# Nine dense layers as one stage, and a state-space model's output matrices made round by round

## The chip, the cores and the metric

The program runs on one core of a Trainium2 chip. The metric is the device time of one execution in microseconds. Names used here: TensorE (PE, with its weight loads PEld), VectorE (DVE), ScalarE (ACT), GpSimd (POOL), and SP, whose queue issues all the DMA.

## The reference

Two blocks of a network run one after the other on 1024 tokens of width 1024, all in float32. The first block puts 16 meta tokens ahead (1040 positions), normalizes, multiplies by a wide input matrix, and runs two mixers: a state-space mixer (s5) and a gated recurrence in heads (hgrn2). What matters here comes after:

```python
y = gelu(y)                                   # end of s5_mixer, its scan included
y_a = y * sigmoid(y @ w_glu)
merged = sigmoid(p5) * (y_a @ w_ssm_proj) + sigmoid(p6) * (y_b @ w_hgrn_proj)
h = h + merged @ w_out
z = rmsnorm(h, ffn_norm_g)
u = causal_dwconv(z @ w_up, conv_w, conv_b)   # 2 x 2816 columns, 3 taps
h = h + (silu(u[..., :2816]) * u[..., 2816:]) @ w_down
return rmsnorm(h[:, 16:], final_norm_g)
```

Inside the state-space mixer, every pair of groups needs the products of powers of its complex decay with its complex output matrix, `a^k * c` for k = 0 to 8. They are the matrix `ca` of the kernel. The second block (pooling, gating, attention, a Fourier mix) is not touched.

## The kernel before

Activations lie transposed: features on the 128 partitions, positions along the free axis, a layer of width 1024 as 8 tiles. Each fp32 product is made from three: operand and weight are split into a high part and a low part, and high x high, low x high, high x low are added up in PSUM. ScalarE writes the high part (a copy), VectorE the low part (a subtraction).

The order of stages around the change: `heads_out` (the projection of the second mixer, with the tables of the scan made beside it), `s5` (the scan), `gather`, nine calls of `dense`, `inverse_rms` between the third and the fourth, then `second_front`, whose names begin with joint. Every stage is a `Phase`: at its end all engines meet and its semaphores are cleared. So no engine begins the next stage until the last has finished.

- `heads_out`: 24 slots (8 output tiles x 3 slices of 342 positions) of 24 matmuls each. Two PSUM banks take turns: slot s waits until VectorE has evacuated slot s - 2 (`moved`). VectorE works through a list `at` that says in which slot each piece of the tables is made: `angles`, `power`, `coefficients`, `scaled_b`, then `outer` 0 to 8, each of six operations on 128 x 512 (all 32 pairs x 16), and `skip` after the last slot. GpSimd makes two turning tables there (`turn_table`, L879 to L884).
- `s5`: four rounds of 8 pairs. TensorE, in order, for round n: `kernel(n+1)`, `turn(n+1)`, `inputs(n+1, 0)`, `inputs(n+1, 1)`, then after `states` of n `outputs(n, 0)`, `inputs(n+1, 2)`, `outputs(n, 1)`. VectorE: `decays(n)`, `weights(n+1)`, `turned_back(n)`, `states_of(n)`. ScalarE copies the kernel blocks (`kernel_out`, L1319) and the transposes (`turn_out`), applies the gelu, and reorders finished tiles (`reorder`, L1349) from chunks to natural order. A tile makes this way through DRAM: stored in chunks, loaded, reordered, stored as `y_glu`. The reorder has two buffers on either side. `inputs(n, 2)` waits until `turned_back(n)` has left its first trip.
- `gather`: loads the 8 tiles of `y_glu` and splits them into the operand `xa`.
- `dense`: mt output tiles in a loop of pairs. Per tile and slice of 342 (or 512 for the down layers, which cover 1024 positions): kt x 3 matmuls. PSUM is two tiles of three banks. Weights have two stages (`stage`, shared by all layers, already loaded for the next layer by `following`), and two buffers for each part (`wh`, `wl`). An epilogue (`epi_...`) works on all the columns of a tile at once. TensorE's loop for a tile begins with these two waits:

```python
pe.wait_ge(low_ready, 2 * i + j + 1)
pe.wait_ge(psum_free, 2 * i + j + 1)
split_matmuls(pe, ps[j], wh[j], wl[j], x[0], x[1], kt, n, first).then_inc(psum_full, 1)
```

The layers in order, with tiles x kt: glu 8x8, ssm_proj 8x8, w_out 8x8, up0 16x8, down0 8x8, up1 16x8, down1 8x8, up2 12x8, down2 8x6. glu, w_out and the down layers read `xa`; ssm_proj and the up layers read `xb`. The up layers all read the same `xb`, so an up layer after a down layer needs nothing from it.

Of the kernel before, what the change touches and what calls it, by code (L numbers as in the profile page):

```python
# [19 lines left out]
P = 128  # L20
# [8 lines left out]
TAU = 8  # L29
# [100 lines left out]
def split_matmuls(pe, ps, wh, wl, xh, xl, kt, n, first):  # L130

    mm = None
    for b, c0, w in pieces(n):
        o = ps[:, 512 * b:512 * b + w]
        for k in range(kt):
            terms = ((wh, xh), (wl, xh), (wh, xl))
            for t, (a, x) in enumerate(terms):
                mm = pe.matmul(o, a[:, k * P:(k + 1) * P], x[:, k, first + c0:first + c0 + w],  # L138
                               start=(k == 0 and t == 0), stop=(k == kt - 1 and t == 2))
    return mm  # L140


def dense(nc, name, weights, mt, kt, x, n, epi, sides=(), side_at=None, store=None, extra=None, steps=(0, 0),
          off=0, stage=None, warm=False, following=None, first=0, pad=0):

    assert mt % 2 == 0
    weights = weights[off:off + mt]
    with Phase(nc, name) as ph:
        places = stage or [ph.sb(f"wstage{j}", (P, kt * P)) for j in range(2)]
        stage = [s[:, 0:kt * P] for s in places]
        early = 16 if warm else 0
        wh = [ph.sb(f"whigh{j}", (P, kt * P), F32R) for j in range(2)]
        wl = [ph.sb(f"wlow{j}", (P, kt * P), F32R) for j in range(2)]  # L160
        side = [[ph.sb(f"side{s}_{j}", (P, n)) for j in range(2)] for s in range(len(sides))]
        out = [ph.sb(f"out{j}", (P, n + pad)) for j in range(2)]
        ps = [ph.ps(f"psum{j}", (P, 1536)) for j in range(2)]
        zeroed = ph.sem("pad_zeroed")
        w_landed = [ph.sem(f"weights_landed{j}") for j in range(2)]
        side_landed = [[ph.sem(f"side{s}_landed{j}") for j in range(2)] for s in range(len(sides))]
        out_stored = [ph.sem(f"out_stored{j}") for j in range(2)]
        high_ready, low_ready = ph.sem("high_ready"), ph.sem("low_ready")
# [10 lines left out]
        act_epi, dve_epi = epi(e)  # L179
        half = mt // 2  # L180
        ns = len(sides)

        with nc.Block() as block:
            @block.sync
            def _(sp):
# [2845 lines left out]
```

## Time and profile before

| | |
|---|---|
| median of 3 runs | 3772.22 us (3770.91 to 3781.7) |
| the profiled execution: time, span | 3772.27 us, 3770.5 us |
| TensorE busy | 3351.4 us, 89% of the span |
| VectorE, ScalarE, GpSimd busy | 1994.3, 930.6, 294.9 us |
| mean granted TensorE clock | 0.935 |
| first matmul of glu, first of the stage after down2 | 1297.44 us, 2425.05 us |

Busy times are sums over the whole span. The granted clock is a share of 2.4 GHz, and in the table of stretches its two levels show as 1.00 and 0.50, or a mixture. A TensorE that is busy is not always one at its peak: records overlap, so work per matmul is better read from counts over a stretch. Times of rows are microseconds from the start of the span.

### The profile page before, as it was taken

The page shows a single profiled execution, that of the slowest core. Times are in us where ns is not written, and L with a number is a line of the kernel's source. Part 1 is how long each engine was busy: PE and PEld are TensorE (multiplying, and loading weights), DVE is VectorE, ACT ScalarE, POOL GpSimd, SP SyncE. Part 2 cuts the span into 40 slices and gives each one's busy share as a digit, 9 for nine tenths or more (in the row PEclk, how much of TensorE's full clock was granted, in tenths as well). Part 3 has the DMA queues.
Part 4 walks back from the last instruction along what each step waited for, and adds up shares of the span by engine and source line. Part 5 has one row for each costly group of instructions (what it writes and reads, how often), then busy time and mean ns, then how long its engine had stood idle before and what let it go on. Part 6 is the DMA issues. An engine that isn't in the chain of part 4 may idle for free. (4 is left out here: it accounts for less than half of the span.)

```text
span 3770.5 us, 48109 instructions
## 1 busy us (share of the span) xinstructions
PE 3351.4 (89%) x19662; PEld 3016.3 (80%) x19662; DVE 1994.3 (53%) x2626; ACT 930.6 (25%) x1143; POOL 294.9 (8%) x327
## 2 busy tenths in 40 slices
PE   3999999997878599899899898899988977999787
PEld 3999999997866499899789788799988974555445
DVE  5566566564877134556246345645445536666236
ACT  3222222222223211121011001222133314444213
POOL 0000000000536000000000000000022001222100
PEclk9999999998988599999999999999989988999998
DMA  2322222322353423311311311411121330000221
GB/s 95 96 87 77 74 91 86 96 85 97 128 61 86 135 95 123 112 45 45 123 50 45 106 67 50 144 41 41 49 82 36 136 127 1 1 1 1 91 77 68
DMA packets 102120, 287.36 MB, mean 76 GB/s; under 512 B 13120, under 2 KB 31936, under 8 KB 101568
## 3 DMA queue, kind: packets, MB, share of 16 engines
q1 hardware_dynamic: 101952, 285.03, 23.4%
q8 instruction: 117, 1.92, 0.2%
q14 instruction: 51, 0.42, 0.0%
HBM read 221.00 MB, written 63.98 MB: 76 GB/s over the span
## 5 line engine op out<-in xcount | busy, mean ns | idle before, releaser
L756 PE MATMUL mixer_in_dense<-mix_z_high,mixer_in_whigh 128*128 128x348 f32 x1344 | 443.6, 330 | 11.3 <-POOL mixer_in_out L593 11.3
L756 PE MATMUL mixer_in_dense<-mix_z_high,mixer_in_wlow 128*128 128x348 f32 x1344 | 436.6, 325 | 0.0
L756 PE MATMUL mixer_in_dense<-mix_z_low,mixer_in_whigh 128*128 128x348 f32 x1344 | 435.8, 324 | 0.0
L1888 PE MATMUL joint_dense<-rst_norms_operand_b_high,joint_whigh 128*128 128x342 f32 (+2 forms) x1056 | 344.9, 327 | 18.2 <-DVEq L2005 10.1
L138 PE MATMUL up_psum<-rst_norms_operand_b_high,up_whigh 128*128 128x342 f32 x1056 | 341.1, 323 | 21.5 <-DVE up_wlow L262 21.5
L1888 PE MATMUL joint_dense<-rst_norms_operand_b_high,joint_wlow 128*128 128x342 f32 (+2 forms) x1056 | 341.7, 324 | 0.0
L1888 PE MATMUL joint_dense<-irst_norms_operand_b_low,joint_whigh 128*128 128x342 f32 (+2 forms) x1056 | 340.6, 323 | 0.0
L138 PE MATMUL up_psum<-irst_norms_operand_b_low,up_whigh 128*128 128x342 f32 x1056 | 339.7, 322 | 0.0
L138 PE MATMUL up_psum<-rst_norms_operand_b_high,up_wlow 128*128 128x342 f32 x1056 | 339.6, 322 | 0.0
L756 PEld LDWEIGHTS mixer_in_dense<-mix_z_high,mixer_in_whigh 128*128 128x128 f32 x1344 | 257.5, 192 | 13.1 <-POOL mixer_in_out L593 11.9
L756 PEld LDWEIGHTS mixer_in_dense<-mix_z_high,mixer_in_wlow 128*128 128x128 f32 x1344 | 256.7, 191 | 0.8
L756 PEld LDWEIGHTS mixer_in_dense<-mix_z_low,mixer_in_whigh 128*128 128x128 f32 x1344 | 256.3, 191 | 0.0
L1888 PEld LDWEIGHTS joint_dense<-rst_norms_operand_b_high,joint_whigh 128*128 128x128 f32 x1056 | 202.3, 192 | 23.8 <-DVEq L2005 8.0
L138 PEld LDWEIGHTS up_psum<-rst_norms_operand_b_high,up_whigh 128*128 128x128 f32 x1056 | 201.8, 191 | 23.3 <-DVE up_wlow L262 23.3
L1888 PEld LDWEIGHTS joint_dense<-irst_norms_operand_b_low,joint_whigh 128*128 128x128 f32 x1056 | 203.2, 192 | 0.0
L1888 PEld LDWEIGHTS joint_dense<-rst_norms_operand_b_high,joint_wlow 128*128 128x128 f32 x1056 | 202.7, 192 | 0.6 <-issue 0.5
L138 PEld LDWEIGHTS up_psum<-rst_norms_operand_b_high,up_wlow 128*128 128x128 f32 x1056 | 201.7, 191 | 0.0
L138 PEld LDWEIGHTS up_psum<-irst_norms_operand_b_low,up_whigh 128*128 128x128 f32 x1056 | 201.0, 190 | 0.0
L138 PE MATMUL down_psum<-first_operand_a_high,down_whigh 128*128 128x512 f32 x352 | 140.9, 400 | 33.6 <-DVE down_wlow L262 33.6
L2357 PEld LDWEIGHTS attn_turned<-all_ident,attn_probs 128*128 128x128 f32 x640 | 75.3, 148 | 94.1 <-DVE attn_turned_probs L2496 36.4
L138 PE MATMUL down_psum<-first_operand_a_low,down_whigh 128*128 128x512 f32 x352 | 141.5, 402 | 0.0
L138 PE MATMUL down_psum<-first_operand_a_high,down_wlow 128*128 128x512 f32 x352 | 139.6, 397 | 0.0
(548 smaller groups left out, 6906.0 us busy)
## 6 DMA issues: line engine op xcount, KB each, us to landing
mixer_in_wstage<-w_in SPq DMA_DIRECT2D x56, 512.0 KB, 4.7
mixer_in_mod_w<-w_mod SPq DMA_DIRECT2D x64, 384.0 KB, 3.6
first_norms_weights<-w_up SPq DMA_DIRECT2D x44, 512.0 KB, 3.5
down_side<-h SPq DMA_DIRECT2D x24, 512.0 KB, 4.2
h<-down_out SPq DMA_DIRECT2D x24, 512.0 KB, 2.9
first_norms_weights<-ab_w_in SPq DMA_DIRECT2D x20, 512.0 KB, 3.5
p<-mixer_in_out SPq DMA_DIRECT2D x16, 528.0 KB, 2.9
first_norms_weights<-w_down SPq DMA_DIRECT2D x16, 512.0 KB, 4.9
```

The lines of the kernel that those rows point to most:

```text
L138: mm = pe.matmul(o, a[:, k * P:(k + 1) * P], x[:, k, first + c0:first + c0 + w], start=(k == 0 and t == 0), stop=(k == kt - 1 and t == 2))
L756: mm = pe.matmul(pd[s % 2][:, 0:W], a[n % 2][:, P * m:P * (m + 1)], z[x][:, m, W * b:W * (b + 1)], start=m == 0 and i == 0, stop=m == DT - ...
L1888: mm = pe.matmul(pd[s % 2][:, 0:wide], a[n % 2][:, P * k:P * (k + 1)], m, start=k == 0 and e == 0, stop=k == DT - 1 and e == 2)
L2357: mm = pe.transpose(o[:, 256 * kk + P * ab:256 * kk + P * ab + P], pr[(2 * s + ab) % 3][:, c0:c0 + P], c["ident"][:, :])
```

## The change

Two edits.

1. `dense`, `gather`, the epilogues and the inverse root after w_out are replaced by one function `dense_flow`, one phase with an unrolled program over all 100 output tiles. Every tile has three slices of 342 positions (340 in the last of a down layer), which go through a ring of six PSUM banks (`RING`). The weight parts have three buffers (`NW`), and their split runs two tiles ahead. At the start of each layer TensorE goes through the six slices of its first two tiles k by k, and waits for operand tile k only when it comes to it (`operand`); in every other tile it goes slice by slice. VectorE evacuates slice by slice and does the rest of the epilogue after the third. The first operand is loaded and split in the same phase. The sums of squares for the inverse root are three fp32 products inside up0, and the root is made per slice.
2. In `heads_out` the output matrices `ca` are made for round 0 alone, in slots 11 to 13, and `skip` in slot 15. The other rounds' are made in `s5` by VectorE, ahead of `weights(n+1)`. The powers and the output matrices are kept in SBUF for that, and `reorder` in `s5` has one buffer on either side instead of two.

```diff
+def outer_part(ch, tt, ca, re, im, cr, ci, n, nq, k, m, t1, t2):
+    pairs, shape = slice(nq * n, nq * (n + 1)), [P, nq, m, SG]
...
+    ch.inc(tt(u, r, a, ALU.mult))
+    ch.do(tt(v, i, b, ALU.mult))
+    ch.do(tt(ca[:, pairs, 0, k:k + m, :], u, v, ALU.add))
+    ch.inc(tt(u, i, a, ALU.mult))
+    ch.do(tt(v, r, b, ALU.mult))
+    ch.do(tt(ca[:, pairs, 1, k:k + m, :], u, v, ALU.subtract))
...
-                       (8, "coefficients", 0), (9, "reverse", 0), (9, "scaled_b", 0), (10, "negate", 0), (10, "outer", 0),
-                       (12, "outer", 1), (13, "outer", 2), (15, "outer", 3), (16, "outer", 4), (18, "outer", 5),
-                       (19, "outer", 6), (21, "outer", 7), (22, "outer", 8), (NS, "skip", 0)):
+                       (8, "coefficients", 0), (9, "reverse", 0), (9, "scaled_b", 0), (10, "negate", 0), (11, "outer", 0),
+                       (12, "outer", 4), (13, "outer", 8), (15, "skip", 0)):
...
-                            ch.do(ts(pw[:, 2, :, :], pw[:, 1, :, :], -1.0, None, ALU.mult))
+                            ch.inc(dve.tensor_copy(ends_re[:, :, :], pw[:, 0, :, :]))
+                            ch.do(ts(ends_im[:, :, :], pw[:, 1, :, :], -1.0, None, ALU.mult))
...
-        a, b = ([ph.sb(f"{n}{j}", (P, T1)) for j in range(2)] for n in ("chunked", "natural"))
+        a, b = ([ph.sb(f"{n}{j}", (P, T1)) for j in range(1)] for n in ("chunked", "natural"))
...
+                def fetch(m):
+                    if m:
+                        sp.wait_ge(moved, m)
+                    sp.dma_start(a[0][:, :], t["y_chunks"][m]).then_inc(landed, 16)
...
                     if n:
                         put(2 * n - 2)
+                        fetch(2 * n - 1)
                         put(2 * n - 1)
                     for par in range(2):
                         sp.wait_ge(stored[par], 16 * TAU * (n + 1))
-                    for m in (2 * n, 2 * n + 1):
-                        sp.dma_start(a[m % 2][:, :], t["y_chunks"][m]).then_inc(landed[m % 2], 16)
+                    fetch(2 * n)
                 put(DT - 2)
+                fetch(DT - 1)
                 put(DT - 1)
...
                 def kernel(n):
                     pe.wait_ge(spread, n + 1)
+                    if n:
+                        pe.wait_ge(outer_ready, n)
...
                     decays(n)
                     if n + 1 < ROUNDS:
+                        for k in (0, TAU):
+                            outer_part(ch, tt, ca, ends_re, ends_im, cr, ci, n + 1, NQ, k, TAU if k == 0 else 1, t1, t2)
+                        dve.sem_inc(outer_ready, 1)
                         weights(n + 1)
```

The core of `dense_flow` (n is a tile, s a slice, b = s % 3; `free(s)` waits for the evacuation of slice s - 6):

```diff
+    W, RING, NW = NM // 3, 6, 3
...
+            @block.sync
+                load(0)
+                for m in range(4):
+                    sp.dma_start(ring[m][:, :], t["y_glu"][m][:, FIRST:FIRST + NM]).then_inc(y_landed[m], 16)
+                    if m == 0:
+                        load(1)
...
+                for n in range(NTILE):
+                    if n and n - 1 in store_at:
+                        put(n - 1)
+                    nxt = [m for m in sided if m > n]
+                    if n and n - 1 in side_at and side_at[n - 1] + 2 < len(sided):
+                        load_side(sided[side_at[n - 1] + 2])
+                    if n + 4 < NTILE + 2:
+                        sp.wait_ge(low_ready, n + 3)
+                        load(n + 4)
...
+            @block.tensor
+                for l, (name, members, kt) in enumerate(layers):
+                    n0, x = start_of[l], reads[name]
+                    six = range(3 * n0, 3 * n0 + 6)
+                    for k in range(kt):
+                        pe.wait_ge(operand, operand_base[name] + k + 1)
+                        if name == "up0" and k == kt - 1:
+                            pe.wait_ge(acc_ready, 1)
+                            square_sum(0)
+                            square_sum(1)
+                        for s in six:
+                            if k == 0:
+                                free(s)
+                                if s % 3 == 0:
+                                    pe.wait_ge(low_ready, s // 3 + 1)
+                            mm = products(s, k, kt, x)
+                            if k == kt - 1:
+                                mm.then_inc(full, 1)
+                    if name == "up0":
+                        pe.wait_ge(rooted, 1)
+                        square_sum(2)
+                    for s in range(3 * n0 + 6, 3 * (n0 + len(members))):
+                        free(s)
+                        if s % 3 == 0:
+                            pe.wait_ge(low_ready, s // 3 + 1)
+                        for k in range(kt):
+                            mm = products(s, k, kt, x)
+                        mm.then_inc(full, 1)
...
+            @block.scalar
+                def high(n):
+                    act.wait_ge(w_landed[n % 2], 16 * (n // 2 + 1))
+                    if n >= NW:
+                        act.wait_ge(full, 3 * (n - NW + 1))
...
+                for s in range(NS):
...
+                    if b == 0 and n + 2 < NTILE:
+                        high(n + 2)
...
+            @block.vector
+                for s in range(NS):
...
+                    if b == 1 and n + 2 < NTILE:
+                        low(n + 2)
...
+                    elif kind == "up":
+                        j = i % 2
+                        dve.wait_ge(full, s + 1)
+                        if n < start_of[3] + 2:
+                            dve.wait_ge(rooted, 2 * b + 2)
+                        mvd.do(tt(v[j][:, at], bank, rms[:, where], ALU.mult))
+                        if b < 2:
+                            continue
...
+                        ch.do(ts(out[j][:, 0:SEQ], v[j][:, 2:], tap(2), tap(3), ALU.mult, ALU.add))
+                        for e in (1, 0):
+                            ch.do(stt(out=out[j][:, 0:SEQ], in0=v[j][:, e:e + SEQ], scalar=tap(e), in1=out[j][:, 0:SEQ],
+                                      op0=ALU.mult, op1=ALU.add))
+                        if j == 0:
+                            dve.sem_inc(conv_ready, 1)
+                        else:
+                            dve.wait_ge(silued, pair_at[n] + 1)
+                            ch.do(tt(out[1][:, 0:SEQ], other[0][:, 0:SEQ], out[1][:, 0:SEQ], ALU.mult))
+                            write(xa, (n - start_of[layer_of[n]]) // 2, seq, out[1][:, 0:SEQ])
```

## Rows read from the trace of the kernel before

**Rows 1.** Stretches: us; busy us of each engine; granted clock; DMA share, GB/s.
```profile
1071.00:1252.00 181.00, 156.35 (x1004) 125.46 (x1003) 113.40 (x128) 59.46 (x116) 75.63 (x104) 0.81 0.37 68
...
1297.00:2416.00 1119.00, 1036.52 (x5958) 986.03 (x5958) 537.33 (x482) 163.07 (x158) 0.00 (x0) 0.95 0.24 82
```
**Rows 2.** Waits of TensorE: who waited for whom, us in total, times, longest.
```profile
PE down_psum L138 <- DVE down_wlow L262: 33.6, 3, 11.4
...
PE up_psum L138 <- DVE up_wlow L262: 21.5, 3, 7.4
...
PE heads_out_dense L1033 <- DVE heads_out_out L1153: 12.3, 5, 4.9
...
PE ffn_rms_sum L315 <- PEq L101: 9.6, 1, 9.6
...
PE w_out_psum L138 <- DVE w_out_wlow L262: 9.1, 1, 9.1
...
PE ssm_proj_psum L138 <- DVE ssm_proj_wlow L262: 7.7, 1, 7.7
```
**Rows 3.** Stretches inside up0 and down0, and glu's first 5.5 us.
```profile
1617.00:1795.00 178.00, 178.00 (x1136) 178.00 (x1135) 108.34 (x95) 31.52 (x29) 0.00 (x0) 1.00 0.13 42
...
1820.00:1897.00 77.00, 77.00 (x336) 62.98 (x335) 15.93 (x13) 6.37 (x6) 0.00 (x0) 1.00 0.38 129
...
1297.00:1302.50 5.50, 5.06 (x18) 5.06 (x19) 1.61 (x2) 2.34 (x2) 0.00 (x0) 0.50 0.57 177
```
**Rows 4.** Timeline of TensorE: start, us, instruction; idle time before it, releaser.
```profile
1297.44 0.65 PE L138 MATMUL glu_psum<-first_operand_a_high,glu_whigh 128*128 128x342 f32 x1 [45.45 <-DVE glu_wlow L262]
...
2425.05 3.75 PE L1833 MATMUL joint_pooled<-first_norms_inverse_rms,all_ones 128*128 128x512 f32 x4 [9.60 <-PEq L101]
```
**Rows 5.** Timeline of ScalarE at the seam between up0 and down0.
```profile
1804.35 2.00 ACT L240 ACTIVATE down_whigh<-first_norms_weights 128x1024 fp32r<-128x1024 f32 x2 [14.20 <-PEq L101]
```
**Rows 6.** Timeline of SP's queue and ScalarE in gather.
```profile
1271.09 10.39 SPq L1459 DMA_DIRECT2D gather_a<-y_glu  x8
...
1274.77 1.08 ACT L1465 ACTIVATE first_operand_a_high<-gather_a 128x1056 fp32r<-128x1056 f32 x1 [7.72 <-DMA gather_a<-y_glu]
```
**Rows 7.** Timeline of SP's queue and ScalarE at the scan's end.
```profile
1258.01 1.44 SPq L1214 DMA_DIRECT2D scan_chunked<-y_chunks  x2
...
1265.13 2.28 SPq L1196 DMA_DIRECT2D y_glu<-scan_natural  x2
...
1263.05 4.00 ACT L1349 ACTIVATE scan_natural<-scan_chunked 128x1056 f32<-128x1056 f32 x2 [6.74 <-DMA scan_chunked<-y_chunks]
```
**Rows 8.** heads_out: TensorE from slot 11 on; one of VectorE's outer products.
```profile
988.40:1055.30 66.90, 55.31 (x312) 0.90 0.22 77
...
1005.16 1.66 DVE L1133 TENSOR_TENSOR s_ca<-heads_out_t 128x512 f32<-128x512 f32 x1
```
**Rows 9.** The scan: timeline of VectorE, TensorE and SP; two stretches of outputs.
```profile
1120.66 1.23 DVE L884 TENSOR_TENSOR scan_wt<-scan_t 128x1024 f32<-128x1024 f32 x1
...
1123.47 0.56 DVE L1413 TENSOR_TENSOR scan_ei<-scan_v,s_w_im 128x396 f32<-128x396 f32 x1
...
1126.83 1.12 PE L1269 MATMUL scan_v<-scan_u,scan_win 128*64 128x132 f32 x16
...
1178.38 0.90 SPq L1196 DMA_DIRECT2D y_glu<-scan_natural  x2
...
1221.31 0.81 PE L1282 MATMUL scan_y<-scan_u,scan_toeplitz 128*128 128x132 f32 x2 [6.44 <-DVEq L1434]
...
1196.40:1205.20 8.80, 8.80 (x50) 6.75 (x48) 4.50 (x9) 1.00 (x2) 0.00 (x0) 0.97 0.00 0
...
1221.20:1252.10 30.90, 30.68 (x96) 23.04 (x96) 0.00 (x0) 2.46 (x6) 0.00 (x0) 0.50 0.26 75
```
**Rows 10.** Timeline of GpSimd in the scan's turning tables.
```profile
1114.68 1.20 POOL L879 TENSOR_TENSOR scan_pool_t<-s_w_re 128x8 f32<-128x8 f32 x1
...
1160.32 0.21 POOL L879 TENSOR_TENSOR scan_pool_t<-s_w_re 128x8 f32<-128x8 f32 x1
```

More of the change, by code:

```diff
@@ L127, in loop @@
         self.n = base + trips * per
[L130 to L140, printed above, removed]
@@ L1444, in _, with flow_tiles @@
                     states_of(n)
-def gather(nc, name, src, x):
-    with Phase(nc, name) as ph:
-        a = [ph.sb(f"a{j}", (P, T1)) for j in range(4)]
-        landed = [ph.sem(f"landed{j}") for j in range(4)]
-        high_ready, low_ready = ph.sem("high_ready"), ph.sem("low_ready")
+def flow_tiles():
+    layers = [("glu", [("glu", m) for m in range(DT)], DT), ("ssm", [("ssm", m) for m in range(DT)], DT),
+              ("out", [("out", m) for m in range(DT)], DT)]
+    first = 0
+    for f, k in enumerate((8, 8, 6)):
+        layers.append((f"up{f}", [("up", 2 * first + i) for i in range(2 * k)], DT))
+        layers.append((f"down{f}", [(f"down{f}", m) for m in range(DT)], k))
+        first += k
+    return layers
@@ new lines, in put @@
+                def put(n):
+                    q, (kind, i) = store_at[n], tiles[n]
+                    first, size = (META, SEQ) if kind.startswith("down") else (FIRST, NM)
+                    sp.wait_ge(out_ready, q + 1)
+                    sp.dma_start(t["h"][i][:, first:first + size], out[q % 2][:, 0:size]).then_inc(out_stored[q % 2], 16)
+                load(0)
[3 more added lines that the diff above has]
+                        load(1)
@@ new lines, in _ @@
+                for m in range(4, DT):
+                    sp.wait_ge(operand, m - 3)
+                    sp.dma_start(ring[m % 4][:, :], t["y_glu"][m][:, FIRST:FIRST + NM]).then_inc(y_landed[m % 4], 16)
+                for n in (2, 3):
+                    sp.wait_ge(low_ready, n - 1)
+                    load(n)
+                load_side(0)
+                load_side(1)
+                for n in range(NTILE):
[7 more added lines that the diff above has]
+                        load(n + 4)
@@ new lines, in _, with low, write @@
+                tt, stt, ts = dve.tensor_tensor, dve.scalar_tensor_tensor, dve.tensor_scalar
+                def low(n):
+                    dve.wait_ge(high_ready, n + 1)
+                    w = kt_of[n] * P
+                    tt(wl[n % NW][:, 0:w], stage[n % 2][:, 0:w], wh[n % NW][:, 0:w].bitcast(F32),
+                       ALU.subtract).then_inc(low_ready, 1)
+                def write(x, m, where, src):
+                    ch.do(split(dve, ch, x[0][:, m, where], x[1][:, m, where], src))
+                    dve.sem_inc(operand, 1)
```

520 lines of the change are left out of this document (217 added, 303 removed).

## The prediction

> **What bounds the kernel now.** I read the table of stretches first. In the nine dense layers (1297 to 2416 us) TensorE is busy 1036 of 1119 us while VectorE is busy 537 and DMA a quarter of the time [rows 1]: TensorE sets this stage's end, and only its idle time, its slow clock and its time per matmul can be shortened. Second, the waits of TensorE [rows 2]: inside the stage they are 7.7, 9.1, 9.6, 21.5 (three times) and 33.6 (three times), 81.5 us in nine pauses, one at each seam between layers and one before the inverse root. Third, the same table over pieces inside one layer [rows 3]: at full clock (2.4 GHz) 1136 matmuls of 342 columns take 178 us, 0.1567 us each; 336 of 512 columns take 77 us, 0.229 each; after a pause 18 matmuls take 5.06 us at half clock (1.2 GHz), 0.281 each. Fourth, the stage's ends [rows 4]: the first matmul of glu starts at 1297.44 after 45.45 idle, the last of down2 ends at 2425.05 - 9.60 = 2415.45. So the stage lasts 1118.0 us.
>
> Ahead of it lie heads_out and the scan. In the scan TensorE is busy 156 of 181 us but at clock 0.81, and VectorE 113 [rows 1]: two engines take turns there, neither has much room.
>
> **The nine layers as one stage.** What goes: eight ends of a phase. At such a seam ScalarE starts splitting the new weights, already landed, only once everybody has finished, 1804.35 where the last matmul ended near 1795.3 [rows 5]. Now weights are split two tiles ahead into three buffers, beside the matmuls, so the pause has no cause left but a late operand. The operand's tail (evacuate, convolve, gate, split) ends before that 1804.35, so it is at most 9 us long. Over it TensorE has seven of eight slices k for the first two tiles, 7 x 18 x 0.157 = 19.7 us (down2: five of six, 14.1). Covered; without that cover each seam would cost up to 9 us again.
>
> The work itself: 4896 matmuls of 342 columns stay, 1056 of 512 become 1584 of about 341. Together 6480 x 0.1567 = 1015.4 us; today's shares are 767 and 242, so the narrower tiles give back 6. One slow start remains, 18 x (0.281 - 0.157) = 2.3. The sums of squares stay, three fp32 products; four records of 512 columns take 3.75 at half clock [rows 4], so I take 3.5 with the short wait for the first inverse root. The roots are now three pairs with a table load each, but beside 2.8 us of matmuls and with slices 1 and 2 needed 3.8 and 7.5 us later. Stage: 1015.4 + 2.3 + 3.5 = 1021.2 against 1118.0, **-96.8**. VectorE's busy share in up is 108 of 178 us [rows 3], 6.8 us per 11.3 us tile; three short evacuations for one long one add some 0.4. Six banks give two tiles of slack, and after a k-by-k start VectorE has two tiles' work (about 15 us) before TensorE needs, 11 us on, the bank of the second tile's first slice. I keep -80 as the poor end (two us per seam), -99 as the good one. The unrolled program adds no row that I can point to; the scan and the mixer before are unrolled too.
>
> The end of the stage: the last evacuation covers a third of the columns, and the last store leaves before the norm's work instead of after it. Of the 9.60 us [rows 4] I take **-2** (0 to -4).
>
> **The gather.** Today eight tiles are loaded and split, the phase ends, weights are loaded, and the first matmul comes 26.35 us after the first load was issued (1271.09) [rows 4, 6]. Now the first weights go out first, and product k starts when tile k is split. The first load lands 3.7 us after issue, eight take 10.4 us to issue, 1.3 each [rows 6]; then 1.1 on ScalarE [rows 6] and 1.3 on VectorE (1.23 for 1024 columns, [rows 9]): 3.7 + 1.3 + 1.1 + 1.3 = 7.4. After that a k costs TensorE 18 x 0.28 = 5.1 us at half clock, and data come every 1.5: no starving. **-19** (-21 to -15).
>
> **The end of the scan.** The buffers of the reorder go from two to one. Today both loads go out at 1258.01, the first lands at 1263.05, two reorders take 4.00, and the stores go out at once; the gather starts 3.7 after the last [rows 7]. Now each of the last three tiles is load (4.2), reorder (2.0), next load: 3 x 6.6 = 20 from 1256.6, plus 3.7: 1280.3. **+9** (+5 with loads of 3 us, +12 with 5).
>
> **heads_out.** Of 54 operations on 512 columns for the outer products 12 of 512 and 6 of 128 remain, early (slots 11 to 13), and the skip matrix moves under the matmuls. From the twelfth slot on, 312 matmuls take 66.9 us [rows 8]; 13 x 24 x 0.1567 is 48.9. The surplus is waits for VectorE's evacuations (12.3 us over the stage [rows 2]) and the half clock after them. The pieces left are still beside GpSimd's tables, where such an operation takes up to 1.66 us [rows 8]; the three slots with them keep about 4 us. **-14** (-18 to -9).
>
> **The scan's rounds.** Three rounds get 12 new VectorE operations each: six of 1024 columns at 1.23 [rows 9] and six of 128, with overlap 7.4 + 1.5 = 8.9 us, ahead of weights and turned_back. In round 0 VectorE idles longer than that: free. In round 1 it does not: weights end at 1121.89 and turned_back follows at once; its first trip's last read of PSUM ends at 1124.03, and will end 8.9 later. TensorE's third inputs wait for that trip; they started at 1126.83 without a wait, 2.8 us after it [rows 9]. So TensorE pauses 6.2 us. How that ends is seen once in this trace: after 6.44 idle at 1221.31 the clock is at half and stays there for the whole 30.9 us of outputs, 15.4 per half against 8.8 at full [rows 9]. If it goes so here: 6.2 + 6.7 for the half + 2.4 until the next kernel products = 15.3, and round 2's own lateness of VectorE (two rounds' 17.8, less slack) is then hidden behind TensorE. If the clock holds: 6.2 + about 5.5 in round 2. Then ScalarE: after a round's gelus its second reorder now waits for a load that SP issues behind eight stores (the put before is at 1178.38 [rows 9]), some 6 us, and the copies of round 3's Toeplitz blocks are queued behind it; TensorE's transposes wait for those: +4.8, and perhaps 7 more at half clock. Sum: 11.7 + 4.8 = 16.5 or 15.3 + 4.8 + 0 to 7. I take **+20**; ends +8 (rounds absorb half) and +32.
>
> GpSimd's first table in that stretch shows 1.20 us for an operation on 8 columns beside VectorE's two-input operations, 0.21 alone [rows 10]. It has one such operation per VectorE operation, so 12 new ones hold it 9 us longer per round; round 3's turned_back, which waits for the last table, would then be late by a few us, inside the +32. The Trainium skill (SBUF — State Buffer, SBUF: two separate sides) says that whichever of the two starts first has the shared port pair for the whole instruction and the other blocks. By that rule, with both rounds' delays added up, the sum would be some 4 us higher; the trace agrees on the single operation.
>
> **Sum.** -96.8 - 2 - 19 + 9 - 14 + 20 = -102.8. The profiled execution took 3772.27 (span 3770.5), the median is 3772.22, so the two can be set equal: 3772.2 - 102.8 = 3669.4, **3669 us**.
>
> **Rivals.** (a) The banks are late: VectorE's burst after each k-by-k start, plus the single v and gate buffers, leave about 4 us at each of nine seams. For it: two tiles complete together and VectorE must do the convolution of both. Against: 15 us of work against 22 us of matmuls. 3669 + 36 = 3705.
> (b) The scan takes the worst of all its branches and GpSimd's table is last: +13, 3682; inside the range.
> (c) The weights or operands are late after all (SP's one queue holds a store's wait ahead of the next weights), so most seams stay: 60 of the 81.5 us come back, 3730 to 3745. Against: a weight load lands two tiles, 22 us, ahead.
> (d) Slower: in a k-by-k start the six banks change every three matmuls. If TensorE idles a little at each change, the clock falls as it does in the scan, and 8 x 144 + 108 = 1260 matmuls cost 0.281 instead of 0.157: +156, 3825. It decides once two thirds of them run at half clock (103 of the 156 us). Against it: the scan's kernel products change place every few matmuls, and the stretch 1071 to 1252 still has 0.81. The Trainium skill (TensorE: Matmul & The Clock Gate, A second HAM failure mode: psum-queue depth-cycling) tells of a kernel whose cycling through banks kept the clock oscillating; no row here shows it for products of 342 columns.
> (e) The change doesn't do what it says, the program stays bound by the same pauses: excluded for the most part, since no phase ends are left in the stage.
>
> **Chances.** Forecast with its own scatter 0.73, (a) 0.12, (b) 0.08, (c) 0.03, (d) 0.03, (e) 0.01. The terms' ends alone would add up to 3642 and 3711, unlikely all together. Leaving out (c), (d), (e), the upper half of (a) and some 6 in 100 at the low end gives 3645 to 3700. A measurement of this kernel can tell about 0.3% (11 us) from no change: all but (d) and (e) are faster by more, 0.96; same 0.01; slower 0.03.
>
> **What would show it.** Right: TensorE has no wait over 3 us between the first glu matmul and the last of down2, and that stage lasts 1017 to 1030 us at clock 0.99 or more; glu starts 7 to 8 us after the first load; heads_out's last 13 slots take about 53 us; the scan shows a new wait of TensorE for VectorE inside round 0's outputs and a longer one before round 3's transposes, and lasts 15 to 30 us more, tail included. Wrong: waits on the banks' semaphore in up layers, low clock in the first 22 us of each layer, or a scan that grows by less than 10 or more than 40.

## The result and the profile after

The changed kernel takes **3683.76 us** (median of 4 runs, 3683.07 to 3684.67) against 3774.57 us of the kernel before on the same chip: ratio 0.9759, 95% interval 0.9744 to 0.9775. The forecast was 3669 with a range of 3645 to 3700. The profiled executions differ by 3681.3 - 3770.5 = -89.2 us of span, and by TensorE's timeline that comes from these parts (first matmuls, the last gelu and the first load of y are the marks):

| part | before | after | change | forecast |
|---|---|---|---|---|
| up to heads_out's first matmul | 926.1 | 928.4 | +2.3 | 0 |
| heads_out, first to last matmul | 129.1 | 119.1 | -10.0 | -14 |
| scan, first matmul to last gelu | 185.7 | 207.2 | +21.5 | +20 |
| last gelu to first load of y | 18.7 | 29.6 | +10.9 | +9 |
| first load to first matmul of glu | 26.4 | 7.0 | -19.4 | -19 |
| nine layers | 1118.0 | 1022.7 | -95.3 | -96.8 |
| stage exit | 9.6 | 6.4 | -3.2 | -2 |
| from the next stage's first matmul to the end | 1345.4 | 1349.4 | +4.0 | 0 |

(The fixed 11.5 us between heads_out and the scan is in neither row.) The first and the last row are scatter: the profiles of the changed kernel and of the twelve below, none of which touches these stages, have heads_out start between 922.7 and 932.5, and the last part takes 1337 to 1349 us. So 6.3 of the 13.6 us by which the sum of the profile misses the forecast belong to no step. The stages between scatter too. In the seven kernels whose scan is that of the changed kernel it takes 207.2 to 212.2 us, and the scan of the kernel before takes 185.7 here and 187.9 in `flow_alone` below; heads_out takes 118.9 to 120.8 in seven kernels with the changed one, 129.1 and 130.5 with the old.

TensorE's waits, of the changed kernel (who waited for whom, total us, times, longest):

```profile
PE flow_dense L1344 <- DVEq L1457: 37.0, 1, 37.0
...
PE scan_turned_and_kernel L1002 <- ACT scan_toeplitz L1070: 17.0, 5, 5.6
...
PE scan_v L1020 <- DVEq L1165: 9.8, 2, 6.5
...
PE heads_out_dense L784 <- DVE heads_out_out L899: 5.0, 4, 3.4
...
PE flow_dense L1344 <- DVE flow_wlow L1436: 0.4, 1, 0.4
```

Against the nine pauses of [rows 2] the layers show one wait of 0.4 us, besides the 37.0 ahead of the stage. The table of stretches (us; busy of PE, PEld, DVE, ACT, POOL; granted clock; DMA share, GB/s), for heads_out from slot 11, a piece behind the scan's new pause, the scan's last outputs, and the whole dense stage:

```profile
990.70:1047.50 56.80, 52.60 (x312) 51.50 (x312) 31.47 (x39) 7.44 (x7) 46.57 (x79) 0.94 0.25 89
...
1127.70:1149.30 21.60, 21.60 (x83) 16.94 (x82) 21.03 (x19) 1.39 (x3) 20.81 (x17) 0.52 0.15 26
...
1235.00:1266.00 31.00, 30.68 (x96) 23.02 (x96) 0.00 (x0) 4.67 (x7) 0.00 (x0) 0.50 0.27 73
...
1302.70:2325.50 1022.80, 1022.30 (x6486) 1020.88 (x6486) 568.55 (x655) 169.38 (x180) 0.00 (x0) 1.00 0.28 95
```

TensorE is busy 1022.3 of 1022.8 us there at clock 1.00, with VectorE at 569: nothing but the count of matmuls is left. The two lines of the scan are at half clock. Timeline of TensorE at the marks and the new waits (start, us, ..., idle before and releaser):

```profile
1006.03 0.65 PE L784 MATMUL heads_out_dense<-heads_out_yb_high,heads_out_whigh 128*128 128x342 f32 x1 [3.40 <-DVE heads_out_out L899]
...
1125.69 2.03 PE L1020 MATMUL scan_v<-scan_u,scan_win 128*64 128x132 f32 x16 [6.50 <-DVEq L1165]
...
1198.43 1.09 PE L1002 MATMUL scan_turned_and_kernel<-all_ident,scan_wt 128*128 128x128 f32 x4 [5.65 <-ACT scan_toeplitz L1070]
...
1201.86 1.54 PE L1002 MATMUL scan_turned_and_kernel<-all_ident,scan_wt 128*128 128x128 f32 x6 [2.34 <-ACT scan_toeplitz L1070]
...
1302.75 0.65 PE L1344 MATMUL flow_dense<-first_operand_a_high,flow_whigh 128*128 128x342 f32 x1 [37.00 <-DVEq L1457]
...
2331.91 2.90 PE L1847 MATMUL joint_pooled<-first_norms_inverse_rms,all_ones 128*128 128x512 f32 x3 [6.42 <-PEq L101]
```

And SP's queue at the end of the scan, where [rows 7] showed two loads and two stores in pairs:

```profile
1270.35 0.43 SPq L945 DMA_DIRECT2D scan_chunked<-y_chunks  x1
...
1277.68 0.32 SPq L940 DMA_DIRECT2D y_glu<-scan_natural  x1
1278.11 0.37 SPq L945 DMA_DIRECT2D scan_chunked<-y_chunks  x1
1284.52 0.32 SPq L940 DMA_DIRECT2D y_glu<-scan_natural  x1
1284.88 0.43 SPq L945 DMA_DIRECT2D scan_chunked<-y_chunks  x1
1291.40 0.32 SPq L940 DMA_DIRECT2D y_glu<-scan_natural  x1
...
1295.72 0.42 SPq L1304 DMA_DIRECT2D flow_side<-y_glu  x1
```

A load (4.3 us from issue to landing), the reorder on ScalarE (2.06) and the issue of its store (0.4) take 1284.88 - 1278.11 = 6.8 us per tile and stand in a row three times; nobody waits there for the store to land. The next stage's first load leaves at 1295.72, and glu starts 7.03 later.

### The profile page after: what moved, and what is told of

Read it like the earlier page. It is cut to its first block and busy times, and to the rows that moved or that the text cites. A ratio compares the mean times of both kernels' runs of the same rounds, so it can differ in the third digit from the quotient of the medians.

```text
span 3681.3 us, 47804 instructions
## 1 busy us (share of the span) xinstructions
PE 3348.9 (91%) x20190; PEld 3059.9 (83%) x20190; DVE 2014.9 (55%) x2795; ACT 930.9 (25%) x1159; POOL 294.2 (8%) x327
## 5 line engine op out<-in xcount | busy, mean ns | idle before, releaser
L1344 PE MATMUL flow_dense<-rst_norms_operand_b_high,flow_whigh 128*128 128x342 f32 x1248 | 399.2, 320 | 0.4 <-DVE flow_wlow L1436 0.4
L1344 PE MATMUL flow_dense<-irst_norms_operand_b_low,flow_whigh 128*128 128x342 f32 x1248 | 398.3, 319 | 0.0
L1344 PE MATMUL flow_dense<-rst_norms_operand_b_high,flow_wlow 128*128 128x342 f32 x1248 | 397.4, 318 | 0.0
L1902 PE MATMUL joint_dense<-rst_norms_operand_b_high,joint_whigh 128*128 128x342 f32 (+2 forms) x1056 | 344.8, 326 | 17.9 <-DVEq L2019 10.1
L1344 PE MATMUL flow_dense<-first_operand_a_high,flow_whigh 128*128 128x342 f32 (+1 forms) x912 | 291.9, 320 | 37.0 <-DVEq L1457 37.0
L1344 PE MATMUL flow_dense<-first_operand_a_low,flow_whigh 128*128 128x342 f32 (+1 forms) x912 | 292.4, 321 | 0.0
L1344 PE MATMUL flow_dense<-first_operand_a_high,flow_wlow 128*128 128x342 f32 (+1 forms) x912 | 291.7, 320 | 0.0
L491 PEld LDWEIGHTS mixer_in_dense<-mix_z_high,mixer_in_whigh 128*128 128x128 f32 x1344 | 258.1, 192 | 13.6 <-POOL mixer_in_out L328 12.3
L1344 PEld LDWEIGHTS flow_dense<-rst_norms_operand_b_high,flow_whigh 128*128 128x128 f32 x1248 | 235.1, 188 | 1.3 <-issue 1.2
L1344 PEld LDWEIGHTS flow_dense<-rst_norms_operand_b_high,flow_wlow 128*128 128x128 f32 x1248 | 235.1, 188 | 0.1
L1344 PEld LDWEIGHTS flow_dense<-irst_norms_operand_b_low,flow_whigh 128*128 128x128 f32 x1248 | 234.5, 188 | 0.0
L1344 PEld LDWEIGHTS flow_dense<-first_operand_a_high,flow_whigh 128*128 128x128 f32 x912 | 172.9, 190 | 37.3 <-DVEq L1457 37.3
```

Of the source, the lines that this page charges most:

```text
L491: mm = pe.matmul(pd[s % 2][:, 0:W], a[n % 2][:, P * m:P * (m + 1)], z[x][:, m, W * b:W * (b + 1)], start=m == 0 and i == 0, stop=m == DT - ...
L1344: mm = pe.matmul(o, w[n % NW][:, P * k:P * (k + 1)], x[h][:, k, where], start=k == 0 and e == 0, stop=k == kt - 1 and e == 2)
L1902: mm = pe.matmul(pd[s % 2][:, 0:wide], a[n % 2][:, P * k:P * (k + 1)], m, start=k == 0 and e == 0, stop=k == DT - 1 and e == 2)
```

## The experiments

All times are medians; each kernel has 4 runs (the last one 5) beside the kernel before on the same chip, and the interval is that of the ratio to it. Profiles are of one execution each.

### The two edits apart

`flow_alone`: the new dense stage, with `heads_out`, `s5` and `keep` of the kernel before. `ssm_alone`: the reverse.

> The one-stage dense layers with heads_out and the scan of the kernel before. If the two edits act one after the other and add up, this run gets heads_out's old 129.1 us back (+10.1 against the changed kernel) and loses the scan's and its tail's 32.4: 3683.8 - 22.3 = 3661 us, flow stage still 1023 us, first glu matmul 7 us after the first load. Rival: the state-space edit is neutral and the changed kernel's scan is longer only because its stage starts earlier: 3680 or more.

> The state-space edit with the gather and the nine dense phases of the kernel before. Additive theory: slower than before by 22, 3774.6 + 22.3 = 3797 us, with the same scan as in the changed kernel (TensorE's waits of 6.5 and 5.65 us in it). Rival (edit neutral): 3775 within 4.

Measured: flow_alone 3659.51 us (ratio 0.9702, 0.9681 to 0.9723), ssm_alone 3798.05 (1.0063, 1.0043 to 1.0084). In flow_alone the scan takes 187.9, its tail 19.2, glu starts 7.4 after the first load and the layers take 1021.4. The edits add up. The dense stage is worth 3659.51 - 3776.82 = -117, and the state-space edit by itself costs +21 to +24: it gives 10 us in heads_out and loses 32 in the scan and its tail.

### What makes the dense stage free of pauses

`late_split`: at each of the eight seams the new layer's first two weights are split after the old layer's last tile; no phase ends come back.

```diff
-                    if b == 0 and n + 2 < NTILE:
+                    if b == 0 and n and n in start_of:
+                        act.wait_ge(full, 3 * n)
+                        high(n)
+                        high(n + 1)
+                    if b == 0 and n + 2 < NTILE and n + 2 not in start_of and n + 1 not in start_of:
                         high(n + 2)
```

(and `low` on VectorE likewise)

> The changed kernel, but at each of the eight seams the weights of the new layer's first two tiles are split only after the old layer's last tile is finished on ScalarE and VectorE (the phase ends stay away). Theory 1 (a seam's pause in the kernel before was the split of the weights queued behind the last epilogue, not the meeting of the engines as such): each seam waits for epilogue tail (0.5 to 8 us) + 1.1 on ScalarE + 1.2 on VectorE, so 3 to 10 us, and starts at half clock where it is long: about +50, 3734 us (+35 to +75). Theory 2 (it was the phase end: drain, meeting, clearing): under +15, 3699 or less.

Measured: 3746.14 (0.993, 0.9911 to 0.9949), the layers 1088.2 instead of 1022.7, +65.5. TensorE at two seams, and the stretch behind the first:

```profile
1403.29 0.63 PE L1344 MATMUL flow_dense<-rst_norms_operand_b_high,flow_whigh 128*128 128x342 f32 x1 [5.38 <-DVE flow_wlow L1440]
...
1797.60 0.62 PE L1344 MATMUL flow_dense<-first_operand_a_high,flow_whigh 128*128 128x342 f32 x1 [8.88 <-DVE flow_wlow L1440]
...
1403.30:1408.30 5.00, 5.00 (x18) 5.00 (x19) 0.98 (x1) 1.50 (x2) 0.00 (x0) 0.50 0.82 297
```

The eight waits are 5.38, 5.51, 7.54, 8.88, 2.50, 8.88, 2.50 and 8.61, together 49.8. Behind seven of the eight the clock stays at half for another 3.9 to 5.9 us, 33 us in all (18 matmuls in 5.00 us instead of 2.8), which costs half of that; 49.8 + 16.5 = 66.3 accounts for the 65.5. Theory 1 holds. Of the nine pauses of [rows 2] eight are at these seams, 71.9 us; the ninth, 9.6, is the inverse root's. So 71.9 - 49.8 = 22 us, some 3 a seam, are left for the phase ends themselves.

`slices`: TensorE takes the first six slices one after the other (`for s, k in ((s, k) for s in six for k in range(kt))`), only the first of them with the waits for each k.

> The changed kernel, but TensorE goes slice by slice in the first two tiles of a layer too; only its first slice is taken k by k. Theory 1 (the k-by-k start over six banks is what covers an operand's tail): after the last matmul of a layer the tail still takes about 3.7 us after glu and ssm_proj, 5.5 after w_out and 8 after an up layer, of which 3.3 are covered: waits of 0.5, 0.5, 2 and three of 5, with 2.3 of half clock after each of the last three, together +25: 3709 us (+15 to +40). Theory 2 (only the merging counts; the order of k is idle): 3684 within 4.

Measured: 3717.16 (0.9853, 0.9831 to 0.9875), the layers 1058.4, +35.7. A seam, and the start of glu:

```profile
1785.68 0.65 PE L1344 MATMUL flow_dense<-first_operand_a_high,flow_whigh 128*128 128x342 f32 x1 [4.17 <-DVEq L1442]
...
1304.70:1325.00 20.30, 15.35 (x48) 12.31 (x49) 11.00 (x9) 10.21 (x10) 0.00 (x0) 0.52 0.74 268
```

The same stretch of late_split, whose glu also starts at 1304.67:

```profile
1304.70:1325.00 20.30, 20.30 (x113) 20.30 (x114) 11.05 (x9) 10.55 (x10) 0.00 (x0) 0.87 0.77 274
```

The six waits at seams with a new operand are 0.68, 0.81, 2.85, 4.17, 4.18 and 5.11 (expected 0.5, 0.5, 2, 5, 5, 5), 17.8 together. What was not expected is glu's start, where the operand's tiles are still being split one by one: four waits of 4.5 us together and half clock until 1324.0, 48 matmuls in 20.3 us. late_split, which starts as the changed kernel does, has 113 there, so it costs 65 x 0.157 = 10 us. With 2.3 of half clock after the three long waits that makes 35. Theory 1 holds, its size at the upper end of the range.

`one_tile`: `six = range(3 * n0, 3 * n0 + 3)`, the k-by-k start over three banks; the slices taken one by one begin three earlier.

> The changed kernel, but the k-by-k start spans three banks (the first tile of a layer), not six. It covers 7 x 9 x 0.157 = 9.9 us of an operand's tail (7.1 before down2) instead of 19.7. The slice-by-slice run measured the tails as its waits plus 3.3: 4.0, 4.1, 6.1, 7.5, 7.5 and 7.5 us. Theory (cover is a count of matmuls against the tail): no wait over 1 us, 3684 us within 4. Rival (the start over two tiles is needed, since VectorE must also evacuate six full banks in time or the weights of the second tile are late): 1 to 3 us at each of eight seams, 3692 to 3708.

Measured: 3682.47 (0.9753, 0.9732 to 0.9774), no change from 3683.76; the layers take 1023.4 and the waits inside the stage add up to 1.3 us. A cover of 9.9 us over tails up to 7.5 is enough.

### The end of the scan

`tail`: er and ei are second buffers of the reorder for tiles 5 and 7.

```diff
+        a, b = [a[0][:, :], flat(ei)], [b[0][:, :], flat(er)]
+        buf = [0, 0, 0, 0, 0, 1, 0, 1]
```

> The changed kernel, but tiles 5 and 7 of the scan's reorder use er and ei (free by then) as second buffers. Theory: the scan's tail (last gelu to first load of y) is a chain of load, reorder, load, so it goes back from 29.6 to 18.7 us and nothing else moves: 3683.8 - 10.9 = 3673 us. Rival: the tail is bound by the stores of the last chunks and by the phase end, and two of its tiles through the same queue gain 4 or less: 3680.

Measured: 3675.25 (0.9736, 0.9715 to 0.9756). The last gelu to the first load takes 24.0 us (29.6 with one buffer): half of what was expected. That the total came within 3 us of the expected 3673 all the same is scatter of other stages. The load of tile 5 was queued behind the 16 chunk stores, which SP issues until 1270.55; issued between their halves (in `best`, below) it brings the tail to 19.4. So the chain is the cause, and SP's queue was a second link in it.

### Where the scan's 21 us come from

`trips`: in rounds 1 and 2 VectorE takes turned_back's first two trips, then the output matrices, the third trip, and the weights last.

> The changed kernel, but in rounds 1 and 2 VectorE takes trips 0 and 1 of turned_back before the output matrices, trip 2 after them, and the weights last. Theory (the 6.5 us pause of TensorE inside round 0's outputs is VectorE's order, and the half clock of the next 33 us is the pause's consequence): no wait over 1 us there, clock 0.95 or more from there to round 3's transposes, -16.6: 3667 us. Rival 1: the pause goes but the clock stays at half anyway: -6.5, 3677. Rival 2: the wait only moves to the matrices or the weights of round 2, now later by 7 us: 3675 to 3684, with a new wait of TensorE for VectorE before the kernel products or the transposes of round 2.

Measured: 3682.88 (0.9762, 0.9741 to 0.9783), no gain: rival 2, with its new wait of 2.68 us before round 2's transposes. TensorE, and two stretches:

```profile
1152.05 0.81 PE L1033 MATMUL scan_y<-scan_u,scan_toeplitz 128*128 128x132 f32 x2 [4.97 <-DVEq L1185]
...
1125.00:1139.00 14.00, 12.01 (x96) 9.84 (x94) 13.50 (x14) 6.22 (x15) 13.37 (x12) 1.00 0.35 77
...
1152.10:1188.00 35.90, 35.90 (x130) 27.61 (x130) 34.48 (x40) 4.89 (x7) 33.71 (x46) 0.50 0.13 23
```

The pause inside round 0's outputs is gone and the clock there is 1.00. But states(1) is late: 4.97 us right before round 1's outputs, and half clock for all of the 36 us behind it. VectorE's list of that round takes 47.3 us (from the decays at 1104.61 to the end of the states at 1151.94), 45.2 in the changed kernel, and TensorE's own work in a round is 37. The 39 us that the expectation below gives VectorE leave out what its operations lose beside GpSimd's table, which is made at the same time. Two instructions of the changed kernel, the same operation in rounds 0 and 1:

```profile
1099.59 1.24 DVE L1178 TENSOR_TENSOR scan_t<-scan_ei,s_w_im 128x1048 f32<-128x1048 f32 x1
...
1142.31 2.10 DVE L1178 TENSOR_TENSOR scan_t<-scan_ei,s_w_im 128x1048 f32<-128x1048 f32 x1
```

`round2_home`: round 2's matrices in heads_out (`(17, "outer", 32), (19, "outer", 36), (21, "outer", 40)`, the number is 16 x round + k), none in the scan's round 1.

> The changed kernel, but the output matrices of round 2 are made in heads_out (slots 17, 19 and 21), not in the scan's round 1. The run before this one showed that putting VectorE's work of round 1 in another order only moves TensorE's pause: in round 1 VectorE has 39 us of work against TensorE's 37. Theory (amount, not order): with 8.9 us less in that round TensorE's pause inside round 0's outputs goes from 6.5 to below 1, the half clock after it too: -16.6, and the three pieces cost heads_out 1 to 3 us: 3684 - 16.6 + 2 = 3669 us. Rival (the half clock belongs to this part of the scan whatever VectorE does): -6.5 + 2, 3679.

Measured: 3682.33 (0.9757, 0.973 to 0.9783). Heads_out takes 121.0 (+1.9, as expected) and the pause in round 0's outputs is gone, yet the scan takes 205.5. TensorE one round later:

```profile
1166.01 0.71 PE L1021 MATMUL scan_v<-scan_u,scan_win 128*64 128x132 f32 x4 [4.76 <-DVEq L1166]
...
1117.00:1143.00 26.00, 26.00 (x185) 20.79 (x184) 24.60 (x27) 6.55 (x15) 24.35 (x32) 1.00 0.31 63
...
1166.00:1186.00 20.00, 19.99 (x77) 15.51 (x78) 18.81 (x20) 3.51 (x4) 18.98 (x20) 0.50 0.08 14
```

Round 3's matrices, which VectorE makes in its round 2 and which the changed kernel hid behind a TensorE at half clock, now stop it for 4.76 inside round 1's outputs, and the clock falls there instead.

`scan_free` and `best`: round 2's matrices stay in heads_out, those of rounds 1 and 3 are both made in the scan's round 0, with turned_back ahead of the weights there; ScalarE's second reorder moved behind the next round's transposes; `best` has the tail's buffers too.

```diff
+                        for q in ((1, 3) if n == 0 else ()):
...
+                        if n:
+                            dve.sem_inc(outer_ready, 1)
+                        else:
+                            turned_back(n)
                         weights(n + 1)
```

> The changed kernel with round 2's output matrices in heads_out, round 1's and round 3's in the scan's round 0 (where VectorE had 10 us idle before turned_back; turned_back stands ahead of the weights there), and ScalarE's second reorder of a round moved behind the next round's transposes. The run before showed that one round with too much VectorE work is enough: with round 2's share gone the pause moved to round 2 (4.8 us, then half clock) and the scan still took 205.5 us from first matmul to last gelu. Theory (every added wait over about 4 us costs itself and some 10 us of half clock, and there is nothing else in the scan's loss): without any of them the scan takes 186 again, as before the change (185.7), against 207.2: 3684 - 21 + 2 for heads_out = 3665 us. Rival: GpSimd's tables or ScalarE's copies take over as the late one: 3675 or more.

> The same, and er and ei as second reorder buffers for tiles 5 and 7, with the load of tile 5 issued between the two halves of the last chunk stores (in the run that used these buffers it stood behind all 16, and the tail took 24.0 us, not 18.7). Theory: tail 19 to 20 us, so 3665 - 10 = 3655 us, below the dense layers alone with the old state-space code (3659.5). Rival: the tail stays at 24: 3659.

Measured: scan_free 3677.92 (0.9741, 0.9719 to 0.9762), scan 204.1, the theory failed; best 3669.68 (0.9735, 0.9709 to 0.9761) and not 3655, scan 201.6, with the tail of 19.4 that was expected. The theory of the "wait over about 4 us" is wrong. scan_free:

```profile
1111.73 0.59 PE L1034 MATMUL scan_y<-scan_u,scan_toeplitz 128*128 128x132 f32 x1 [2.89 <-DVEq L1188]
...
1111.80:1149.00 37.20, 37.20 (x134) 28.57 (x135) 31.23 (x33) 2.79 (x6) 34.92 (x48) 0.50 0.16 28
...
1149.00:1158.00 9.00, 9.00 (x64) 7.53 (x62) 2.66 (x4) 3.80 (x9) 7.59 (x28) 0.80 0.25 70
```

Right before the outputs stands a wait of 2.89 us, and half clock for the whole 37 us behind it. It isn't shown that 2.89 us do this by themselves: in both kernels a wait of 4.01 us ends 12 us earlier, before the transposes, the clock is at half after that one too, and it has been back for only 3.4 us when it falls again. No run has so short a wait alone there. ScalarE's part did work: before round 3's transposes TensorE waits 3.00 again, not 5.65 and 2.34.

`no_pause`: `best` with the changed kernel's order in round 0 (matrices, weights, turned_back).

> As the run before with all parts (round 2's matrices in heads_out, the others' in round 0, ScalarE's second reorder later, er and ei as buffers, early load of tile 5), but VectorE's order in round 0 is again that of the change: matrices of rounds 1 and 3, then the weights, then turned_back. There the scan still took 201.6 us (204.1 without the buffers), though no wait of TensorE before the last round was over 4.01 us: turned_back ahead of the weights had put a wait of 2.9 to 3.3 us right before round 0's outputs, and the clock stood at half for the 36 us behind it. Theory (what costs is a pause right before or inside the outputs, of 2.9 us as well as of 6.5; a wait of 3.0 before the transposes gives the clock back within 7 us): with none in rounds 0 to 2 the stretch from round 0's outputs to round 1's Toeplitz wait lasts 40 us at clock over 0.9, the scan 187 us: 3670 - 14.5 = 3655 us. Rival (the amount of VectorE work moved into round 0 is the cause, by a later states(0)): the same wait stands before round 0's outputs again, scan over 198 us, 3667 or more.

Measured: **3651.53** (5 runs, 3643.67 to 3655.1; ratio 0.9661, 0.9644 to 0.9677), scan 188.3, tail 19.2, heads_out 121.5. The theory holds. The amount of VectorE work is that of `best`, and only the place of the wait differs:

```profile
1091.73 0.49 PE L1030 MATMUL scan_v<-scan_u,scan_win 128*64 128x132 f32 x2 [4.86 <-DVEq L1177]
...
1096.00:1103.00 7.00, 7.00 (x60) 5.93 (x58) 6.71 (x9) 3.30 (x8) 0.00 (x0) 0.98 0.00 0
...
1114.00:1148.00 34.00, 31.23 (x225) 25.10 (x222) 31.44 (x33) 9.50 (x23) 32.04 (x39) 0.95 0.24 48
```

TensorE waits 4.86 us ahead of round 0's third inputs, followed by the kernel products: clock 0.98 within 5 us. Its outputs have no wait ahead, and 34 us with them pass at 0.95. The wait before round 1's transposes differs too, 4.01 us in best and 3.00 here, as in the changed kernel. This kernel beats the change and also flow_alone; the intervals of its ratio and of flow_alone's (from 0.9681) don't meet. Its scan and tail are back at flow_alone's (187.9 and 19.2), and it keeps 9 us in heads_out (121.5 against 130.5).

### heads_out

`spread`: round 0's three pieces in slots 11, 13, 15, the skip matrix in 17.

> The changed kernel, but heads_out's three output-matrix pieces of round 0 stand in slots 11, 13 and 15 and the skip matrix in 17, not in 11, 12, 13 and 15. Theory: the missing 4 us of heads_out (56.8 us from slot 11 on, not 52.9) are the queue of two pieces of 5 and 7 us in slots that last 3.8 each: the waits of 3.4 and 0.7 go, with the half clock after them: -5, 3679 us. Rival: beside GpSimd's tables every piece is longer than two slots, and the waits only move: 3684.

Measured: 3680.45 (0.9758, 0.9737 to 0.9779; single runs 3670.77 to 3686.32); heads_out 118.3 against 119.1, less than the scatter. The rival: the waits moved. Two of VectorE's instructions there and TensorE's wait after them:

```profile
1004.96 1.54 DVE L654 TENSOR_TENSOR heads_out_t<-s_powers_re,s_c_im 128x512 f32<-128x512 f32 x1
...
1008.00 2.18 DVE L806 TENSOR_TENSOR heads_out_wlow<-heads_out_wstage,heads_out_whigh 128x1024 fp32r<-128x1024 f32 x1
...
1010.75 0.62 PE L784 MATMUL heads_out_dense<-heads_out_yb_high,heads_out_whigh 128*128 128x342 f32 x1 [2.95 <-DVE heads_out_out L899]
```

Beside GpSimd's table the split of a weight takes 2.18 us (1.23 alone), so a slot's own work grows as well as the piece.

## Why the prediction was right, point by point

- **The nine layers as one stage** (-96.8, measured -95.3): right in mechanism and size. 6480 x 0.1567 = 1015.4 is what a busy TensorE does; 7.3 us remain for the slow start, the sums and 0.4 of waiting, where I had 5.8. That split weights two tiles ahead take away the seam is shown (late_split, +65.5), that the k-by-k start covers the operand's tail too (slices, +35.7), and the cover has room (one_tile, 0). Rivals (a), (c), (d) and (e) are excluded: no bank waits, no late weights, clock 1.00 through the stage, starts over six banks included. (The Trainium skill, in TensorE: Matmul & The Clock Gate, A second HAM failure mode: psum-queue depth-cycling, tells of a clock that went up and down while matmuls cycled through banks; it was named beside (d), and no run here shows it.)
- **Stage exit** -3.2 (forecast -2) and **gather** -19.4 (-19): inside their ranges, the gather as worked out; 7.0 us from load to matmul against 7.4.
- **The scan's rounds** (+20, measured +21.5): the first pause is 6.50 (forecast 6.2). From round 1's third inputs, which stand inside round 0's outputs, to round 2's transposes the scan lost 10.1 us to half clock (forecast 9.1). Round 2's lateness hid behind it, as assumed, and round2_home shows it uncovered. Before round 3's transposes the waits are 5.65 and 2.34 instead of 2.99: +5.0 (forecast 4.8). All three steps stand. That the terms agree so closely is luck in part: in the seven kernels with this scan the first pause is 5.04 to 6.76 us and the scan grows by 19 to 27. That half clock costs more than the pause was already in the sum; the experiments add where a pause brings it. The working on GpSimd was off: 12 operations at 0.99 us each are 11.9 us a round, not 9, and the two tables together took 91.6 us instead of 80.8. They were done at 1197.52, and round 3's turned_back began at 1208.52, released by TensorE, so they made nothing late there. What the sum had not seen is VectorE's side, its operations of up to 2.1 us instead of 1.24.
- **The scan's end** (+9, measured +10.9): three cycles, to the end of the last store's issue, took 1291.72 - 1270.35 = 21.4 us instead of 20, the first landing 5.2 us after issue and not 4.2, and the first load of y follows by 4.0 us, not 3.7; the first weights of glu are issued ahead of it. The stated bound of 15 to 30 us for scan and tail together was 2 us too narrow (32.4).
- **heads_out** (-14, measured -10.0): right in sign, mis-sized by 4. I kept 4 us for the three slots with pieces; they cost 56.8 - 48.9 = 7.9. The pieces took 5.0, 6.8 and 5.5 us. The last was thought small, six operations on 128 columns. Three of them, and two of GpSimd's at that time:

```profile
1006.40 0.28 DVE L651 TENSOR_TENSOR heads_out_t<-s_powers_negated_im,s_c_im 128x128 f32<-128x128 f32 x1
1006.72 1.26 DVE L652 TENSOR_TENSOR s_ca<-heads_out_t 128x128 f32<-128x128 f32 x1
1008.01 1.10 DVE L653 TENSOR_TENSOR heads_out_t<-s_powers_negated_im,s_c_re 128x128 f32<-128x128 f32 x1
...
1006.41 1.41 POOL L616 TENSOR_TENSOR s_w_re<-heads_out_pool_t 128x512 f32<-128x512 f32 x1
1007.90 1.06 POOL L617 TENSOR_TENSOR heads_out_pool_t<-s_w_re,s_w_im 128x512 f32<-128x512 f32 x1
```

The same form takes 0.28 alone, and the last four of the piece take 1.10 to 1.33. Each of these ends 0.14 to 0.16 us after one of GpSimd's operations does, so there one operation of VectorE costs as much as one of GpSimd's (1.06 to 1.41 us), and their number counts, not their columns. In the sum I had charged a small one as small. The Trainium skill (SBUF — State Buffer, SBUF: two separate sides) has the shared port pair locked for whole instructions, by whichever of the two engines starts first; the trace agrees, by those 0.14 to 0.16 us. In slot 11, where GpSimd's operations take 0.41 to 0.95 us, six operations of VectorE on 512 columns take 0.76 to 0.90 (0.69 alone).
- **Rival (b)**, the scan at its worst with GpSimd's table last, was priced at 3682, nearer to the 3684 measured than the forecast itself. It isn't what happened: the scan grew by 21.5 us, not by 33, and the table was not the last to be ready. The total lies there by the sum of small misses.
- **The total**: -102.8 forecast, -90.8 by medians, -89.2 by profile. Of the 13.6 us between forecast and profile, 6.3 are scatter outside the change, 4.0 heads_out, 1.9 the tail, 1.5 the scan, 1.5 the layers, less 1.6 for exit and gather. All but the 1.6 lie on the same side, and there was room for them in the range. (The ends of the terms add up to 3643 and 3712, not 3642 and 3711.) The two edits are of opposite sign, which the sum of their terms had (-118 for the dense edit, +15 for the other; measured -114 to -117 and +21 to +24).

Open: why the outputs keep the clock at half. The runs show that they do after every wait right before or inside them, of 2.89 to 6.76 us, in the changed kernel and in all that share its scan, in trips, round2_home, scan_free and best, and that the same products without such a wait run at full clock; what in them does it was not tried. The 3 us per phase end are a difference of two runs whose seams differ in more than that.

## What to carry to other kernels

Where stages of matmuls follow each other, first look for what is queued behind the last epilogue (here the split of the next weights); moving it ahead and taking the new operand k by k over three banks closes the seam, and how much cover is needed is a count of matmuls against the operand's tail. Work moved off a full engine goes into a list of idle times by round, with the amount per round as well as the order: a round with 45 us of work against 37 can't be saved by reordering. Take the length of that work from the trace, with what runs beside it. And price a pause by what TensorE runs behind it: 6.5 us inside the outputs cost 16.6, 4.9 in front of the third inputs and the kernel products cost about 2 more than themselves (4.6 us at half clock).

## What the runs showed of the hardware that was not expected

- The granted clock after a pause depends on the work behind it: 6.50 us idle inside the scan's outputs (chained products of 132 columns) left it at 0.50 for 23 us, until 5 us into the kernel products; 2.89 us right before them, with 4.01 us 12 us earlier, for 37 us; 4.86 us before the third inputs and the kernel products, back at 0.98 within 5 us; 3.00 us before the transposes, back 3 to 10 us behind the wait. It is not the products alone: without a wait ahead the outputs ran at 0.95 to 1.00.
- A VectorE operation on two inputs beside GpSimd's table can take about 1 us more than alone, whatever its width: 128 columns took 1.26 us there and 0.28 alone, 512 columns up to 1.66 [rows 8] and 0.69 alone, a split of 1024 2.18 against 1.23. Where GpSimd's operations are long, the two engines end theirs in turn, 0.14 to 0.16 us apart.
- Stages that no kernel here changes differ between profiles by up to 10 us (when heads_out begins) and 12 us (from the stage after down2 to the end). Differences under 5 us were therefore read from marks inside a stage, not from the total.
